# Forget gate and keys of a bidirectional recurrence by exponentials and logarithms, in place of a half tanh and a GpSimd product

## What is computed

```python
def forget_gate(f_logits, lb):
    f = lb + (1.0 - lb) * jax.nn.sigmoid(f_logits.astype(jnp.float32))
    return split_heads(jnp.log(f)), split_heads(1.0 - f)

# in gla_scan, by chunks of tokens, b = cumsum(log f):
k_dec = kc * jnp.exp(b_last - b)
new_state = exp(b_last) * state + einsum('bhck,bhcv->bhkv', k_dec, vc)
o = einsum(q * exp(b), state) + einsum(scores(q, k, decay), v)
```

## Time and profile before

| | |
|---|---|
| median of 3 runs | 2297.72 us (2297.08 to 2298.5) |
| the profiled execution | 2297.26 us, span 2295.4 us |
| busy over the span | PE 2170.8 (95%), DVE 1590.8 (69%), ACT 1038.6 (45%), POOL 499.6 (22%) |
| recurrence, first `gate` to last `exps` | 552.6 to 941.2 us of the span |
| busy in it | PE 368.37, DVE 296.67, ACT 258.96, POOL 253.18 of 388.60 us |

### The profile page before, as it was taken

One profiled execution on the slowest core, in us unless ns is written; L12 is line 12 of the kernel. 1 busy time (PEld: TensorE's weight loads), 2 busy tenths in 40 slices (PEclk: granted clock), 3 DMA queues, 4 the chain that ended last, 5 costly groups with the idle time before them and its releaser, 6 DMA issues. The chain is left out here.

```text
span 2295.4 us, 38798 instructions
## 1 busy us (share of the span) xinstructions
PE 2170.8 (95%) x14917; PEld 1453.6 (63%) x14917; DVE 1590.8 (69%) x2230; ACT 1038.6 (45%) x1333; POOL 499.6 (22%) x538
## 2 busy tenths in 40 slices
PE   7799999999999999899966999999999999999995
PEld 3444444444878787645525777777777777777772
DVE  2749999784679687765565666766666666766666
ACT  3611011455666666545542444454444444553444
POOL 1710001012657566300021111101111011101111
PEclk9899999999999999899978999999999999999998
DMA  9431002454020221375545677666676677667676
GB/s 348 99 73 35 17 23 88 140 170 127 6 56 13 82 57 24 117 266 173 170 166 193 209 242 228 232 225 220 221 239 223 214 232 237 227 222 232 222 238 266
DMA packets 216932, 377.16 MB, mean 164 GB/s; under 512 B 38147, under 2 KB 79619, under 8 KB 216333
## 3 DMA queue, kind: packets, MB, share of 16 engines
q1 hardware_dynamic: 198702, 317.38, 40.8%
q0 software_dynamic: 16528, 56.47, 9.1%
q10 hardware_dynamic: 1616, 2.16, 0.3%
HBM read 313.44 MB, written 62.54 MB: 164 GB/s over the span
## 5 line engine op out<-in xcount | busy, mean ns | idle before, releaser
L90 PE MATMUL pgu<-xlo,mwhi 128*128 128x256 bf16 x2048 | 558.3, 273 | 0.0
L89 PE MATMUL pgu<-xhi,mwhi 128*128 128x256 bf16 x2048 | 558.3, 273 | 0.0
L91 PE MATMUL pgu<-xhi,mwlo 128*128 128x256 bf16 x2048 | 558.3, 273 | 0.0
L2470 DVE TENSOR_TENSOR mwlo<-mwst,mwhi 128x2048 bf16<-128x2048 f32 x187 | 427.0, 2283 | 0.0
L2367 ACT ACTIVATE mwhi<-mwst 128x2048 bf16<-128x2048 f32 x186 | 350.8, 1902 | 0.0
L2375 ACT ACTIVATE thb<-pgu 128x256 f32<-128x256 f32 x128 | 49.0, 383 | 547.4 <-PE pgu L91 547.3
L690 DVE SCALAR_TENSOR_TENSOR co<-u,taps,co 128x1984 f32<-128x1984 f32 (+22 forms) x120 | 234.1, 1951 | 3.7
L2481 DVE SCALAR_TENSOR_TENSOR thb<-thb,pgu 128x256 f32<-128x256 f32 x128 | 53.8, 420 | 258.2 <-ACT thb L2375 258.2
L2303 POOL TENSOR_TENSOR mpflag<-mpflag 1x1 f32<-1x1 f32 x46 | 37.5, 815 | 846.2 <-DVE ysb L2497 579.3
L89 PEld LDWEIGHTS pgu<-xhi,mwhi 128*128 128x128 bf16 x2048 | 200.4, 98 | 24.5
L90 PEld LDWEIGHTS pgu<-xlo,mwhi 128*128 128x128 bf16 x2048 | 200.4, 98 | 24.5
(11 more groups left out here) (400 smaller groups left out, 4326.9 us busy)
## 6 DMA issues: line engine op xcount, KB each, us to landing
mwst<-in_w_gate SPq DMA_DIRECT2D x32, 2048.0 KB, 8.9
mwst<-in_w_up SPq DMA_DIRECT2D x32, 2048.0 KB, 7.9
mwst<-in_w_down SPq DMA_DIRECT2D x32, 2048.0 KB, 7.9
wst<-in_w_in SPq DMA_DIRECT2D x28, 512.0 KB, 5.9
big<-in_ada_w SPq DMA_DIRECT2D x5, 2048.0 KB, 13.9
s_rows<-row SPq DMA_DIRECT2D x16, 520.0 KB, 5.8
u<-in_ada_w SPq DMA_DIRECT2D x8, 1024.0 KB, 6.1
xt<-in_x SPq DMA_DIRECT2D x16, 512.0 KB, 4.4
```

The lines of the kernel that those rows point to most:

```text
L89: nc.tensor.matmul(out, lh, rh, start=(first and k == 0), stop=False)
L90: nc.tensor.matmul(out, lh, rl, start=False, stop=False)
L91: ins = nc.tensor.matmul(out, ll, rh, start=False, stop=(last and k == n - 1))
L2470: nc.vector.tensor_tensor(wlo[:, b, ks], wst[:, b % NS, ks], whi[:, b, ks], ALU.subtract)\
```

## The change

The key is now made first, from z by functions of exponential and logarithm alone, all on ScalarE: with y = 40 - relu(40 - z) = min(z, 40) and G = ln(1 + exp(y)), the key is KK = exp(ln(1-lb) - G), and log f = ln(1 - KK). The relu is there to cap z at 40. ln(1-lb) of all heads is made once at the start of the stage (tile `lnk`). So `gate` has three activations where it had one, `logs` two where it had one, `keep` on POOL is gone with its flag, `lh` has one column in place of three, and `gb` with its DVE operation in `conv_stage` is gone.

```diff
-                nc.vector.tensor_scalar(GW_.gh[:], GW_.lbd[:], -0.25, 0.25, ALU.mult, ALU.add).then_inc(GW_.lb_ok, 1)
-                nc.vector.tensor_scalar(GW_.gb[:], GW_.lbd[:], 0.25, 0.75, ALU.mult, ALU.add).then_inc(GW_.lb_ok, 1)
+                nc.vector.tensor_scalar(GW_.gh[:], GW_.lbd[:], -0.5, 0.5, ALU.mult, ALU.add).then_inc(GW_.lb_ok, 1)
...
-                def keep(h, i):
-                    h, i = at(h, i)
-                    p, n, d = i % 2, size(i), UNITS[i][0]
-                    wait(pool, th_ok, U(h, i) + 1)
-                    if i < 2:
-                        wait(pool, hd_ok, h * 6 + 3 * i + 3)
-                    wait(pool, kt_ps, U(h, i - 1))
-                    wait(pool, pf_ok, U(h, i) + 1)
-                    nc.gpsimd.tensor_tensor(pflag[:], pflag[:], pflag[:], ALU.mult).then_inc(pf_ok, 1)
-                    nc.gpsimd.tensor_scalar(KK[:, p, 0:n], G[:, p, 0:n], -1.0, lh[:, d, 2:3], ALU.add, ALU.mult).then_inc(kk_ok, 1)
...
                     wait(act, pj_ps, U(h, i) + 1)
                     wait(act, kk_ok, U(h, i - 1))
-                    wait(act, lf_ok, U(h, i - 1))
-                    nc.scalar.activation(G[:, p, 0:n], pj[p][:, 0:n], ACT.Tanh, scale=0.5).then_inc(th_ok, 1)
+                    g = G[:, p, 0:n]
+                    nc.scalar.activation(g, pj[p][:, 0:n], ACT.Relu, bias=capz[:, 0:1], scale=-1.0).then_inc(th_ok, 1)
+                    wait(act, th_ok, U(h, i) + 1)
+                    nc.scalar.activation(g, g, ACT.Exp, bias=capz[:, 0:1], scale=-1.0).then_inc(ez_ok, 1)
+                    wait(act, ez_ok, U(h, i) + 1)
+                    nc.scalar.activation(g, g, ACT.Ln, bias=1.0).then_inc(sp_ok, 1)
 
                 def logs(h, i):
                     h, i = at(h, i)
                     p, n, d = i % 2, size(i), UNITS[i][0]
-                    wait(act, th_ok, U(h, i) + 1)
+                    wait(act, sp_ok, U(h, i) + 1)
                     if i < 2:
-                        wait(act, hd_ok, h * 6 + 3 * i + 3)
+                        wait(act, hd_ok, h * 2 + i + 1)
+                    wait(act, kt_ps, U(h, i - 1))
+                    nc.scalar.activation(KK[:, p, 0:n], G[:, p, 0:n], ACT.Exp, bias=lh[:, d, 0:1], scale=-1.0).then_inc(kk_ok, 1)
+                    wait(act, kk_ok, U(h, i) + 1)
                     wait(act, at_ps, X(h, i - 1))
                     wait(act, qi_ok, X(h, i - 1))
-                    nc.scalar.activation(E[:, p, 0:n], G[:, p, 0:n], ACT.Ln, bias=lh[:, d, 1:2], scale=lh[:, d, 0:1])\
-                        .then_inc(lf_ok, 1)
+                    nc.scalar.activation(E[:, p, 0:n], KK[:, p, 0:n], ACT.Ln, bias=1.0, scale=-1.0).then_inc(lf_ok, 1)
...
+                wait(act, cap_ok, 1)
+                wait(act, GW_.lb_ok, 4)
+                nc.scalar.activation(lnk[:], GW_.gh[:], ACT.Ln).then_inc(lnk_ok, 1)
                 gate(0, 0)
...
                 def constants(h, d):
-                    wait(dve, lf_ok, U(h, d - 1))
                     wait(dve, kk_ok, U(h, d - 1))
-                    nc.vector.tensor_copy(lh[:, d, 0:1], gh[:, d, bass.ds(h, 1)]).then_inc(hd_ok, 1)
-                    nc.vector.tensor_copy(lh[:, d, 1:2], gb[:, d, bass.ds(h, 1)]).then_inc(hd_ok, 1)
-                    nc.vector.tensor_scalar(lh[:, d, 2:3], gh[:, d, bass.ds(h, 1)], -1.0, None, ALU.mult).then_inc(hd_ok, 1)
+                    nc.vector.tensor_copy(lh[:, d, 0:1], lnk[:, d, bass.ds(h, 1)]).then_inc(hd_ok, 1)
```

More of the change, by code:

```diff
@@ L390, in __init__ @@
         self.gh = m.sb("gh", [P, 2, HEADS])
-        self.gb = m.sb("gb", [P, 2, HEADS])
+        self.lnk = m.sb("lnk", [P, 2, HEADS])
         self.ng = m.sb("ng", [P, HEADS])
@@ L933, in heads_stage @@
         whi, wlo, wst = GW_.hi, GW_.lo, GW_.st
-        gh, gb, ng = GW_.gh, GW_.gb, GW_.ng
+        lnk, ng = GW_.lnk, GW_.ng
+        CAP_Z = 40.0
         qT = m.sb("qT", [P, T])
@@ L950, in heads_stage @@
         se = m.sb("se", [P, 2, ST, SMW])
-        lh = m.sb("lh", [P, 2, 3])
+        lh = m.sb("lh", [P, 2, 1])
+        capz = m.sb("capz", [P, 1])
         ngh = m.sb("ngh", [P, 1])
@@ L959, in heads_stage @@
         flag = m.sb("hflag", [1, 1])
-        pflag = m.sb("hpflag", [1, 1])
         pout = K["pout"]
@@ L968, in heads_stage @@
         at0_ok = m.sem("at0_ok")
-        hd_ok, pf_ok, ng_ok = m.sem("hd_ok"), m.sem("pf_ok"), m.sem("ng_ok")
+        hd_ok, ng_ok, cap_ok, lnk_ok = m.sem("hd_ok"), m.sem("ng_ok"), m.sem("cap_ok"), m.sem("lnk_ok")
+        ez_ok, sp_ok = m.sem("ez_ok"), m.sem("sp_ok")
         w_in, w_hi, w_lo = GW_.loaded, GW_.hi_ok, GW_.lo_ok
@@ L1087, in _ @@
                 nc.gpsimd.memset(segm[:], 1.0).then_inc(msk_ok, 1)
-                nc.gpsimd.memset(pflag[:], 0.0).then_inc(pf_ok, 1)
+                nc.gpsimd.memset(capz[:], CAP_Z).then_inc(cap_ok, 1)
                 wait(pool, msk_ok, 1)
@@ L1136, in low @@
                     nc.gpsimd.tensor_tensor(ml[:, j % 2], of[:, j], mh[:, j % 2], ALU.subtract).then_inc(hml_ok, 1)
-                keep(0, 0)
-                keep(0, 1)
                 wait(pool, zero_ok, 1)
@@ L1147, in one @@
                             decay_k(h, i + 1)
-                        if there(i + 2, prev, cur, nxt):
-                            keep(h, i + 2)
                         for r, j in due(h, i, 11, prev, cur):
@@ L1415, in read @@
                         .then_inc(hm_ok, 1)
+                wait(dve, lnk_ok, 1)
                 for d in range(2):
```

## The result

The changed kernel takes **2377.14 us** (median of 4 runs, 2375.68 to 2378.82) against 2297.4 for the kernel before, run beside it: a ratio of 1.0353, 95% interval 1.034 to 1.0366, or +79.7 us. Its profiled execution has a span of 2376.6 us, 81.2 longer than that of before. The forecast was 2400 in a range of 2374 to 2432, so the sign was right and the size too large by 23 us.

A forecast was written before the change was run, and what follows sets the result against it. PE was taken to bound the kernel, with ScalarE taking over after the change; a 22.9 us head and 468.2 us of loop put the last `se` 102.8 us later, so 2297.26 + 102.8 = 2400 us, range 2374 to 2432.

The forecast's parts named there:

- PE bounds the stage, with 3.2 us of slack on ScalarE a unit: Recurrence before the change: PE busy 368.37 of 388.6 us, ScalarE idle 129.6 us over 40 units.
- The removed GpSimd operations give nothing: GpSimd's two operations a unit and VectorE's small copies: removing them gains nothing, as both engines have idle time.
- Four loads a unit, 162 in the stage: ScalarE's table loads: 162 in place of 80, the 82 added at 1.283 us costing 105.2 us.
- The rival of one table: Exp and Ln share one table, almost no loads, PE keeps the pace: 2277 to 2297 us, say 2290; chance 0.04.
- The activations: Added ScalarE activation work: 1.98 us a unit of 512 columns, 1.35 of 256, 74.2 us in all.
- A step of 11.7, by its four parts: ScalarE's 512-column step: logs 4.0, wait for sums 2.3, on to the exponential of se 2.0, gate 3.4 us.
- The delay beside GpSimd, 0.3 of 1.1 us: VectorE's scan and small copy slowed while GpSimd works: 0.3 of 1.1 us kept, making the step 12.0 us.
- the six steps of 256: Loop steps of 256 columns: savings in logs, gate, scan and subtraction make them 9.9 us each, 59.4 in all.
- Finished segments, 2.16 us each: Squares, inverse root and cast at 0.62 each plus 0.3 for mean_log on ScalarE's path, 12 times: 25.9 us.
- PE has 1.9 us of slack, so the gate doesn't wait: PE's projection is done at 18.4 us, the gate needing it stands at 20.3; PE idles 1.65 us a step.
- The clock rival: PE's idle gaps lower TensorE's clock, making steps 14.5 us and the kernel 2495 us; chance 0.10.
- The head of the stage: Work ahead of the loop from 552.6 us: 22.9 us, so step 0 starts at 575.5 in place of 565.19.

The follow-up runs named there:

- spread_2: one_set plus two table loads a unit, at the start of logs and ahead of the forget gate's logarithm: 2331.63 us, ratio 1.0157.
- one_set_gp: one_set with a pair of GpSimd operations like the removed ones put back in every unit, on an unread scratch tile: 2297.95 us, ratio 1.0015.
- one_set: Changed kernel with one load of the table holding both Exp and Ln ahead of the stage's first logarithm: 2285.17 us, 0.9952 of the kernel before.
- one_set_3: one_set plus three table loads in a bunch behind the gate's logarithm in every unit, ahead of a finished segment's squares: 2414.67 us, ratio 1.0517.
- the spread kernels: one_set plus two, three or four table loads a unit, spread over ScalarE's step: 2331.63, 2372.98 and 2423.42 us.

## Why the prediction was right, and where it was off

- *PE bounds the stage, with 3.2 us of slack on ScalarE a unit.* Right: with the loads gone PE sets the pace again, and the activations cost nothing. But the slack is an average: two loads a unit, 2.6 us, cost 46.5 us (`spread_2`).
- *The removed GpSimd operations give nothing.* Wrong where PE sets the pace: there they are worth 11 to 14 us (`one_set_gp`). Whether they give anything where ScalarE does was not tested.
- *Four loads a unit, 162 in the stage.* Right, count and length: 162 x 1283 ns. The rival of one table is false for the change as it stands, but the premise of its rule holds. The Trainium skill says in "ScalarE: Activation LUTs", section "Table sets: the hidden batching unit", that a set holds both functions; `one_set` bears that out with one load in the stage. What the built program doesn't do of itself is to choose that set. And the rival's time for one load, 2290, was 5 us off.
- *The activations.* The rows shown differ from their terms by 10 ns or less, and ACT is busy for 431.7 us, 438.4 predicted.
- *A step of 11.7, by its four parts.* Right within 0.1 us: 11.6.
- *The delay beside GpSimd, 0.3 of 1.1 us: wrong, it is nothing.* I had worked out that GpSimd would be done before the next scan and took 0.3 all the same, against my own sum. In the step shown above GpSimd works from 1010.11, the end of exp(-B), to 1016.26, and the next scan starts at 1018.60. With the 0.1 above, a step was 0.4 us too long: 32 x 0.4 = 12.8 us, and 9.5 in place of 9.9 in the six steps of 256, 2.4.
- *Finished segments, 2.16 us each: too much.* The work for one is spread over two steps of 12.0 to 12.7 us, which together are 0.9 to 1.6 us longer than two plain ones of 11.6. `mean_log` hides wholly in the waits for the sums and the chain, and squares, inverse root and cast start some 0.1 us before the end of their neighbours, so each adds 0.52 and not 0.62 (the inverse root of 0.61 starts at 1010.71, the gate at 1011.23). That is about 7 us in 12 steps.
- *PE has 1.9 us of slack, so the gate doesn't wait.* Right for all but 3.0 us, with one step of 14.5 us at 840 to 855 in which the gate waited 1.78 us. The granted clock fell to 0.94 in the stage (0.98 before), and cost only that: elsewhere a slower PE still came before the gate. The clock rival can be seen ahead of that one step: PE had waited 0.91 and 1.31 us for GpSimd's keys, and its granted clock was 0.50 from 836 to 840. `one_set_3` shows that the rival was a real one: 3.55 us of standstill in the wrong place, and it was there.
- *The head of the stage.* Step 0 starts at 575.33, forecast 575.5.

The three oversized terms make 12.8 + 2.4 + 7 = 22.2 us; the slow step gives some back. The loop from step 0 to the last `se` took 447.3 us (575.33 to 1022.67), forecast 468.2, 20.9 less. The last `se` is 81.7 us later than before, and the span 81.2.

## What to carry to other kernels

Count the table loads in the built program before believing that two functions share a table, and name the set that holds both ahead of the stage: here it was worth 92 us of 2377. An engine with slack takes added work for nothing until its own step in program order is as long as the bounding engine's, and from there on each microsecond costs a microsecond in each step; so write out the step part by part rather than take a share of the busy time. Do it for the short steps and those with extra work too: two loads that the plain step swallowed cost 46.5 us in the others. Before putting work ahead of a short operation, look who waits for it: three loads ahead of a 0.6 us square cost 36 us more than the same three behind it.

## What I had not expected of the hardware

- A table load takes 1283 ns whatever it replaces. The loads of the spread kernels name the table that is already there, and a plain step still grew by 1.3 us for each; the next activation starts 0.01 us after a load ends (1012.67 + 1.28, then 1013.96).
- The delay of VectorE beside GpSimd depends on whether the two meet, and so on which engine sets the pace. The same scan has a mean of 1515 ns before, 1429 in `one_set` and 1224 in the changed kernel, whose GpSimd operations are those of `one_set`; the 128x16 copy has 967, 333 and 177.
- An idle gap on PE can cost twice. In `one_set_3` 3.55 us of waiting are followed by matmuls of 1.87 in place of 1.05 us, and only then does the engine that caused the gap have to wait for PE.
